# The experts' stage of a hybrid encoder: combination behind the next item's first gate unit, gather in two halves, no zero tile, one-hot turn after the head

## What is computed

```python
gate = sum(one_hot(top_idx, 8) * softmax(top_val)[..., None], axis=-2)   # (256, 8), two entries a token
for e in range(8):
    out = out + gate[..., e:e+1] * ((silu(h @ w_gate[e]) * (h @ w_up[e])) @ w_down[e])
```

## Time and profile before

| what | value |
|---|---|
| median of 3 runs | 1934.15 us |
| span of the profiled execution, first to last instruction | 1931.6 us |
| experts' stage, first gate unit to the last combination | 887.85 us to 1917.93 us of the span |
| weights read | 470.46 MB, 244 GB/s over the span |
| share of the chain that ended last | PE 73%, DVE 17%, POOL 4%, issue 4%, ACT 2%, DMA 0% |

### The profile page before, as it was taken

How to read it: one execution, slowest core, us unless ns; L and a number is a source line. 1 busy time by engine, 2 the same in 40 slices (tenths; PEclk the granted TensorE clock), 3 DMA queues, 4 the chain that set the end, 5 groups by cost and what they waited for, 6 DMA issues and landing times.

```text
span 1931.6 us, 27830 instructions
## 1 busy us (share of the span) xinstructions
PE 1790.1 (93%) x10438; PEld 1558.8 (81%) x10438; DVE 1520.9 (79%) x1465; ACT 1033.9 (54%) x790; POOL 359.4 (19%) x404
## 2 busy tenths in 40 slices
PE   3787998999998989989999999999999999999997
PEld 3776898999997778888878878878778788788785
DVE  6699857454557999466988979979889799798897
ACT  3222443334333224445766767767667677676675
POOL 5875714920000556120000000000000000000000
PEclk7898998999998889998999999999999999999999
DMA  7333354555553333544999989989989899899893
GB/s 210 97 100 110 131 182 135 173 176 182 187 176 107 102 117 111 180 158 169 370 344 321 369 296 363 374 291 373 339 317 375 295 363 374 289 371 349 305 378 122
DMA packets 256346, 472.26 MB, mean 244 GB/s; under 512 B 14134, under 2 KB 104486, under 8 KB 256294
## 3 DMA queue, kind: packets, MB, share of 16 engines
q1 hardware_dynamic: 249091, 468.82, 69.2%
q0 software_dynamic: 608, 2.10, 0.4%
q10 hardware_dynamic: 6595, 0.62, 0.3%
HBM read 470.46 MB, written 1.05 MB: 244 GB/s over the span
## 4 chain that ended last, share of the span: by engine, by line
PE 73%; DVE 17%; POOL 4%; issue 4%; ACT 2%; DMA 0%; POOLq 0%; DVEq 0%; ACTq 0%
PE ps L1561 11%; PE ps L1563 11%; PE ps L1562 11%; PE ps L1332 6%; PE ps L1334 6%; PE ps L1333 6%; PE ps L1573 5%; PE ps L1575 5%; PE ps L1574 5%; DVE fp L739 5%; DVE fp L742 3%; DVE wlo L228 3%; PE ps L1543 2%; DVE fp L971 2%; PE ps L1634 2%
## 5 line engine op out<-in xcount | busy, mean ns | idle before, releaser
L228 DVE TENSOR_TENSOR wlo<-raw,whi 128x2048 fp32r<-128x2048 f32 x446 | 1034.5, 2330 | 248.0 <-ACT whi L222 246.3
L222 ACT ACTIVATE whi<-raw 128x2048 fp32r<-128x2048 f32 x448 | 857.5, 1914 | 326.3 <-PE ps L1334 183.8
L1332 PE MATMUL ps<-fr,whi 128*128 128x256 f32 x1760 | 507.2, 288 | 16.7 <-DVE fr L739 8.9
L1333 PE MATMUL ps<-fr,whi 128*128 128x256 f32 x1760 | 502.8, 286 | 0.0
L1334 PE MATMUL ps<-fr,wlo 128*128 128x256 f32 x1760 | 502.3, 285 | 0.0
L1332 PEld LDWEIGHTS ps<-fr,whi 128*128 128x128 f32 x1760 | 343.2, 195 | 29.8 <-issue 25.0
L1561 PE MATMUL ps<-whi,fr 128*128 128x512 f32 x896 | 357.0, 398 | 1.2 <-DVE fr L739 1.2
L1563 PE MATMUL ps<-whi,fr 128*128 128x512 f32 x896 | 349.4, 390 | 0.0
L1562 PE MATMUL ps<-wlo,fr 128*128 128x512 f32 x896 | 348.5, 389 | 0.0
L1333 PEld LDWEIGHTS ps<-fr,whi 128*128 128x128 f32 x1760 | 343.1, 195 | 0.2 <-issue 0.2
L1334 PEld LDWEIGHTS ps<-fr,wlo 128*128 128x128 f32 x1760 | 342.6, 195 | 0.0
(11 more groups left out here) (211 smaller groups left out, 1321.5 us busy)
## 6 DMA issues: line engine op xcount, KB each, us to landing
raw<-in_moe_w_gate SPq DMA_DIRECT2D x112, 1024.0 KB, 7.3
raw<-in_moe_w_up SPq DMA_DIRECT2D x112, 1024.0 KB, 7.0
raw<-in_moe_w_down SPq DMA_DIRECT2D x112, 1024.0 KB, 6.9
raw<-in_w_in SPq DMA_DIRECT2D x44, 1024.0 KB, 5.1
raw<-in_dense_w_gate SPq DMA_DIRECT2D x14, 1024.0 KB, 5.0
raw<-in_dense_w_up SPq DMA_DIRECT2D x14, 1024.0 KB, 5.0
raw<-in_dense_w_down SPq DMA_DIRECT2D x14, 1024.0 KB, 5.0
raw<-in_w_conv_out SPq DMA_DIRECT2D x8, 1024.0 KB, 5.2
```

The lines of the kernel that those rows point to most:

```text
L222: act.activation(whi[:, slot % SPL, :], raw[:, slot, :], ACT.Copy).then_inc(hi_ready, 1)
L228: dve.tensor_tensor(wlo[:, slot % SPL, :], raw[:, slot, :], whi[:, slot % SPL, :].bitcast(F32), ALU.subtract).then_inc(lo_ready, 1)
L1332: pe.matmul(o, w_h, x_h, start=first, stop=False, skip_group_check=True)
L1333: pe.matmul(o, w_h, x_l, start=False, stop=False, skip_group_check=True)
```

## The change

The combination of an item is no longer at its end but in the next item, behind gate 0; the last item's stands behind the loop. The gather is cut into two halves with turn_hidden between them. The zero tile, its semaphore and its two matmuls are gone; the first down products of an item are written with start=True. PM is turned behind up 1 and not behind gate 0. On VectorE the adds move in front of silu_step in the next item's head, the choice of the next tokens into the first turn of blocks, and one split_lo ahead of xg_lo. On ScalarE one split_hi moves ahead of the last thi_step, and the copies of PT into the first turn. For this the first item is written out ahead of the loop, and in every item the first of the six inner turns is written out too. The semaphore waits of the diff that only change their counts are left out here.

```diff
 ScalarE
-                for j in range(4):
                     if j == 1:
+                        thi_step(item * NB + r)
+                    if j == 2:
+                        tanh_step(item * NB + (r + 1), mm + 6)
+                    split_hi(act, MOE0 + j + 6, item * NB + r)
+                    if j == 2 and isinstance(r, int):
                         act.wait_ge(e_pt_ps, item + 1)
                         act.activation(PT, ps[:, 7, 0:256], ACT.Copy).then_inc(e_pt, 1)
                         act.activation(gslot[:, :], ps[:, 7, 256:257], ACT.Copy).then_inc(e_pt, 1)
...
+                expert_block(item, m, 0)
+                with act.Fori(1, NB - 1) as r:
+                    expert_block(item, m, r)
+                split_hi(act, MOE0 + ITEM, item * NB)
                 thi_step(item * NB + (NB - 1))
                 act.wait_ge(e_xg_ps, item + 2)
                 act.activation(FR[:, 0:1024], ps[:, 5:7, :].rearrange("p a n -> p (a n)"), ACT.Copy).then_inc(e_xgh, 1)
-                for j in range(2):
-                    split_hi(act, MOE0 + ITEM + j, item * NB)
+                split_hi(act, MOE0 + ITEM + 1, item * NB)
 VectorE
+                    split_lo(dve, MOE0 + j + 6, item * NB + r)
+                    if j == 2 and isinstance(r, int):
+                        dve.wait_ge(e_pt_ps, item + 1)
+                        select_tokens(bass.ds(item + 1, 1))
...
                 for j in range(4):
-                    if j == 1:
-                        dve.wait_ge(e_pt_ps, item + 1)
-                        select_tokens(bass.ds(item + 1, 1))
+                    if j == 2 and not first:
+                        dve.wait_ge(e_acc, (item - 1) * 4)
+                        add_products(item - 1)
                     if j == 2:
                         silu_step(item * NB)
                     split_lo(dve, MOE0 + j + 2, item * NB)
...
                 hid_step(item * NB + (NB - 1), m + (ITEM - 2))
                 tlo_step(item * NB + (NB - 1))
+                split_lo(dve, MOE0 + ITEM, item * NB)
                 xg_lo(item + 2)
-                for j in range(2):
-                    split_lo(dve, MOE0 + ITEM + j, item * NB)
+                split_lo(dve, MOE0 + ITEM + 1, item * NB)
 TensorE
                     expert_product(m + j, (MOE0 + j) % RAW, 0 if name == "g" else 1, i)
-                    if j == 0:
-                        pe.wait_ge(e_acc, item * 4)
-                        for h in range(TH):
-                            pe.transpose(ps[:, 7, P * h:P * h + P], PM[:, h, :], ident[:, :])
-                        pe.matmul(ps[:, 7, 256:257], PM[:, 0, :], gcur[:, 0:1], start=True, stop=False)
-                        pe.matmul(ps[:, 7, 256:257], PM[:, 1, :], gcur[:, 1:2], start=False, stop=True).then_inc(e_pt_ps, 1)
-                pe.wait_ge(zero_ready, 1)
-                pe.wait_ge(e_y, item)
-                for j in range(2):
-                    pe.matmul(ps[:, 3 + j, :], zeroR, xgH[:, 0:4, :], start=True, stop=False, skip_group_check=True)
+                    if j == 0 and not first:
+                        combine(item - 1)
+
+                if not first:
+                    pe.wait_ge(e_acc, item * 4)
+                for h in range(TH):
+                    pe.transpose(ps[:, 7, P * h:P * h + P], PM[:, h, :], ident[:, :])
+                pe.matmul(ps[:, 7, 256:257], PM[:, 0, :], gcur[:, 0:1], start=True, stop=False)
+                pe.matmul(ps[:, 7, 256:257], PM[:, 1, :], gcur[:, 1:2], start=False, stop=True).then_inc(e_pt_ps, 1)
+
+                expert_block(item, m, 0)
+                with pe.Fori(1, NB - 1) as r:
+                    expert_block(item, m, r)
...
-                gather(item + 2)
+                gather_half(item + 2, 0)
                 turn_hidden(q0 + (NB - 1))
+                gather_half(item + 2, 1)
                 for i in range(2):
                     expert_down(m + (ITEM - 2 + i), (MOE0 + ITEM - 2 + i) % RAW, q0 + (NB - 1), i, last=(i == 1))
-                pe.wait_ge(e_y, item + 1)
-                pe.wait_ge(e_pt, item * 2 + 2)
-                pe.wait_ge(e_xgl, item + 2)
-                for k, bank in enumerate(COMB_BANKS):
-                    pe.matmul(ps[:, bank, :], PT[:, P * (k // 2):P * (k // 2) + P], ysc[:, 512 * (k % 2):512 * (k % 2) + 512],
-                              start=True, stop=True).then_inc(e_comb, 1)
+            expert_item(0, first=True)
+            with pe.Fori(1, n_over + E) as item:
+                expert_item(item)
+            pe.wait_ge(e_xgl, n_over + (E + 1))
+            combine(n_over + (E - 1))
```

More of the change, by code:

```diff
@@ L694, in _, with expert_item @@
                         act.activation(gslot[:, :], ps[:, 7, 256:257], ACT.Copy).then_inc(e_pt, 1)
+            def expert_item(item):
+                m = item * ITEM + MOE0
+                for j in range(4):
                     if j == 2:
@@ L715, in _ @@
                                scale=gslot[:, 0:1]).then_inc(e_y, 1)
+            expert_item(0)
+            with act.Fori(1, n_over + E) as item:
+                expert_item(item)
             for h in range(TH):
@@ L1254, in _, with silu_step @@
             n_over = dve.value_load(meta[0:1, 0:1], min_val=0, max_val=3)
[L1255 to L1272, removed]
-                    if j == 1:
+            def silu_step(q):
+                dve.wait_ge(e_tanh, q + 1)
+                stt(sgM, tgM, 1.0, ps[:, 0, :], ADD, MUL).then_inc(e_silu, 1)
@@ new lines, in hid_step, with tlo_step, add_products @@
+            def hid_step(q, n):
+                dve.wait_ge(unit_used, n)
+                dve.wait_ge(e_silu, q + 1)
+                stt(hhM, sgM, 0.5, ps[:, 1, :], MUL, MUL).then_inc(e_hid, 1)
+            def tlo_step(q):
+                dve.wait_ge(e_thi, q + 1)
+                tt(FR[:, 2560:3072], ps[:, 2, :], FR[:, 2048:2560].bitcast(F32), SUB).then_inc(e_tlo, 1)
+            def add_products(item):
+                for k, bank in enumerate(COMB_BANKS):
+                    dve.wait_ge(e_comb, item * 4 + (k + 1))
+                    a = acc[:, k // 2, 512 * (k % 2):512 * (k % 2) + 512]
+                    tt(a, a, ps[:, bank, :], ADD).then_inc(e_acc, 1)
@@ L1274, in _, with expert_block @@
+            def expert_block(item, m, r):
+                mm = m + r * 6
+                for j in range(6):
+                    if j == 0:
+                        hid_step(item * NB + r, mm + 4)
+                    if j == 1:
+                        tlo_step(item * NB + r)
+                    if j == 2:
+                        silu_step(item * NB + (r + 1))
+                    split_lo(dve, MOE0 + j + 6, item * NB + r)
+                    if j == 2 and isinstance(r, int):
                         dve.wait_ge(e_pt_ps, item + 1)
@@ L1276, in _, with expert_item @@
                         select_tokens(bass.ds(item + 1, 1))
+            def expert_item(item, first=False):
+                m = item * ITEM + MOE0
+                for j in range(4):
+                    if j == 2 and not first:
+                        dve.wait_ge(e_acc, (item - 1) * 4)
+                        add_products(item - 1)
                     if j == 2:
@@ L1536, in turn_residual, with gather_half @@
                 ins.then_inc(xa_ps, 1)
-            def gather(count):
+            def gather_half(count, half):
                 pe.wait_ge(e_sel, count * 3)
-                for c in range(KC):
+                for c in range(4 * half, 4 * half + 4):
                     for h in range(TH):
-                        ins = pe.matmul(ps[:, 5 + c // 4, P * (c % 4):P * (c % 4) + P], htok[:, h, c * P:c * P + P],
+                        ins = pe.matmul(ps[:, 5 + half, P * (c % 4):P * (c % 4) + P], htok[:, h, c * P:c * P + P],
                                         PM[:, h, :], start=(h == 0), stop=(h == TH - 1))
-                ins.then_inc(e_xg_ps, 1)
+                if half == 1:
+                    ins.then_inc(e_xg_ps, 1)
             turn_residual(0)
             pe.wait_ge(ht_ready, 4)
-            gather(1)
+            gather_half(1, 0)
+            gather_half(1, 1)
             for b in range(1, 4):
@@ L1572, in expert_down @@
                         o, c, cols = ps[:, 3 + j, :], 2 * i + k, slice(512 * j, 512 * j + 512)
-                        pe.matmul(o, tH[:, c, :], wh[:, k, cols], start=False, stop=False, skip_group_check=True)
+                        pe.matmul(o, tH[:, c, :], wh[:, k, cols], start=first and k == 0, stop=False, skip_group_check=True)
                         pe.matmul(o, tH[:, c, :], wl[:, k, cols], start=False, stop=False, skip_group_check=True)
@@ L1583, in turn_hidden, with combine, expert_block, expert_item @@
                 ins.then_inc(e_t_ps, 1)
-            with pe.Fori(0, n_over + E) as item:
+            def combine(item):
+                pe.wait_ge(e_y, item + 1)
+                pe.wait_ge(e_pt, item * 2 + 2)
+                for k, bank in enumerate(COMB_BANKS):
```

(18 more changed lines are left out.)

76 lines of the change are left out of this document (23 added, 53 removed).

## The result

The changed kernel takes 1910.8 us (median of 4 runs, 1910.37 to 1912.87), the kernel before 1934.77 us in the same comparison. The ratio is 0.9872, 95% interval 0.986 to 0.9884: 1.3% faster (the two medians alone give 0.9876). The forecast was 1911.2 us.

The account below looks back on a forecast made before the run. TensorE's matmuls bound the kernel inside items, leaving time to win only at boundaries. Savings of 7.8 + 11.5 + 3.7 = 23.0 us from 1934.15 gave 1911.2 us, range 1906 to 1917.

Parts of the forecast that it names:

- Part one: Item boundary, gather in two halves around the transposes: down units start 0.97 us earlier, eight times, 7.8 us.
- The new wait: Last transposes, behind the gather's first half: 0.69 us wait for VectorE's hidden values, which the whole gather had covered.
- Part two: Combination behind the next item's gate 0: gate 0 fills TensorE's 1.64 us wait for ysc in seven items, 11.5 us.
- Part three: Zero tile removed: its two matmuls no longer delay the next gate unit by 0.46 us, eight times, 3.7 us.
- Part four: Work moved elsewhere (PM's turn, adds, splits, token choice, copies of PT): cost 0, bound 1 us an item.
- VectorE becoming late: Rival, 11%: VectorE's spare time overdrawn by 1 us in seven items, TensorE waits ahead of first turn of blocks; 1918 us.
- The loads: Rival, 4%: DMA loads become the bound; if 341 GB/s were all there is, the whole gain goes, 1934 us.
- The fetches: Rival, 3%: TensorE's longer loop over items stalls for code fetches at seven returns, some 5 us each; 1946 us.
- That more comes back: Rival, 5%: without stalls and with the 0.69 us wait hidden, up to 0.8 us an item more; 1905 us.
- That it does nothing: Rival, 2%: the waits move with the parts, for instance ysc late for gate 0's end; 1930 to 1934 us.

## Why the prediction was right

**The bound.** TensorE inside the items, waits only at the boundary: the trace after has TensorE without a gap in the items as before, and the zero tile, the whole gather and the wait for ysc, each put back, lengthened the item by about what they take of its time.

**Part one, 0.97 us an item; measured 1.09, and 1.12 when it was undone.** The new wait came, of 0.60 us from start to start (half the gather is 1.78, and the transposes start 2.38 behind its start) and not 0.69. I had taken VectorE's way to TensorE at 0.15 us from the lower part's row; for the hidden values it was 1384.49 - 1384.43 = 0.06. The second half took 1.71 and not 1.78. That the lateness of the hidden values was the end of the chain is shown by the version with them first, which took 0.61 us an item away. In the changed kernel the second half ended with the chain of lower steps, as worked out: the lower part ends at 1385.81 + 0.69 = 1386.50, the down matmuls start at 1386.69 and wait for nothing. The upper bound of this part was a little low: with the hidden values first, the way from the gather's start to the down units is 5.67 - 3.92 = 1.75 us shorter than before, and not at most 1.66.

**Part two, 1.64 us in seven items; measured 1.72 when combination and adds were undone together.** The mechanism is the one stated, and the combination itself took 3.44 us instead of 3.51 (from 1394.96 to 1398.40, which is one distance of 0.23 ahead of the row at 1398.63, as the forecast took 1404.67 from 1404.90). The two make 1.71. What the prediction had not seen is that the two moves of this part need each other. It costed the adds' new place at nothing, and it is nothing, but only because the combination in the same head gives VectorE 3.4 us of TensorE's time. With the combination alone put back that cover is gone and 0.95 us an item appears.

**Part three, 0.46 us; measured 0.48 with the tile back.**

**Part four, nothing.** The forecast's 0.4 us or more was the time from the end of the fifth unit's split to TensorE's need, with PM's turn left out. That split ends near 1403.79 + 2.24 = 1406.03, and PM's turn starts at 1406.60: 0.57, so this was about right. The 1.9 us that the five additions showed hold two more terms: PM's turn (1407.18 - 1406.60 = 0.58) and the 0.83 that VectorE waits ahead of the split, together near 2.0. The forecast had 0.4 for the last one (silu to 1409.8, ScalarE's copy to 1410.2), mostly because it took 0.69 for each add, and four in a row take 2.47. ScalarE's and VectorE's earlier split cost nothing and gained 0.10. The other moves of this part (PM's turn, the copies of PT, the choice of tokens) were not undone one by one; parts one to three as measured make 1.09 + 1.71 + 0.48 = 3.28 us, and the item became 3.27 shorter, so no cost is left for them.

**The sum.** 23.0 us were forecast. The item's length fell by 3.27 us and not by 3.07, the experts' stage by 24.6 us in the two profiled executions, the median by 24.0. The small excess is the 0.12 us of part one and the 0.07 of the combination: eight times 0.12 and seven times 0.07 make 1.5. That the forecast of 1911.2 lies within 0.4 us of the median is in part luck: the kernel before had a median of 1934.77 us in the comparison and not 1934.15, and the gain was 1.0 larger, and these two cancel in part. The forecast span of 1908.6 us was 2.5 too short against 1911.1, since the part ahead of the experts took 4.1 us more in that execution. The distance of 2.55 from span to median was not a property of the kernel either: each run of the changed kernel lies 1.8 us above its own span.

**The rivals.** VectorE becoming late in the head did not happen in the changed kernel, but that limit is near: it appears with five more additions, and when the combination is taken from the head. The loads never made anybody wait: no row of waits in the changed kernel's stage names a DMA, and the stretch of 1272 us to 1384 us moved 356 GB/s, above the 349 that the shorter item asks for. The fetches did not come: from 1150 us on the changed kernel has no packet of q8, and a text of over 1100 matmul and weight-load instructions a pass changed nothing. The Trainium skill (Runtime: NRT & Kernel Launch, Instruction fetch mechanics) has a rule that a taken branch beyond a window of two pages forces a fetch before execution goes on. For TensorE the runs speak against it: four such returns with over 1100 instructions in between, and no packet. They agree with the larger memory of 128 KiB that the same section gives this engine, though no run here reaches its size. That more comes back, with the wait for the hidden values gone, did not happen in the changed kernel; the version with the hidden values first did it by one more exchange and took 1906.58 us, near the 1905 of that rival. That it does nothing is ruled out by the item's length.

## What to carry to other kernels

A result that a later step needs on another engine should be followed by a unit of independent work of the same engine, longer than the hand-over: here gate 0 with 2.7 us over 1.6. Before a step is moved to a place of its own, look what the neighbours at the new place live on: the adds were free in the head only beside the combination. And where a queue in order holds both a long job and a short one on which the bound waits, the short one goes first; that single exchange gave another 0.61 us an item.

## What was not expected of the hardware

The hand-over from VectorE to TensorE showed 0.15 us ahead of the down matmul (kernel before) and 0.06 us ahead of the transposes (changed kernel). And four VectorE operations of 0.69 us each in a row, reading PSUM, took 2.47 us together, about 0.60 from one start to the next; the five additions of the test, which read no PSUM, took 3.09 together, 0.60 apart as well. In the old place the adds stood 0.86 apart, each behind the matmuls of its bank (kernel before):

```profile
1403.15 0.69 DVE L739 TENSOR_TENSOR fp<-fp,ps 128x512 f32<-128x512 f32 x1 [0.17 <-PE ps L1634]
...
1404.01 0.69 DVE L739 TENSOR_TENSOR fp<-fp,ps 128x512 f32<-128x512 f32 x1 [0.17 <-PE ps L1634]
```
